# Loading token tile 1 of x from the ACT queue beside tile 0 on the SP queue

## The reference

```python
def rmsnorm(x, g):
    y = x * rsqrt(mean(x * x, -1) + EPS)
    return y * g

xn = rmsnorm(h, pool_norm[0])                # h is x, (256, 2048)
pooled = multiscale_pool(xn)                 # causal means over 2, 4, 8, 16 tokens, minus xn, per 512 columns
y = einsum('bsgc,gce->bsge', pooled, pool_w[0]) + pool_b[0]
h = h + y.reshape(B, S, D) * pool_scale[0]
h = h + swiglu(rmsnorm(h, ffn_norm[0]), w_gate[0], w_up[0], w_down[0])
```

## Time and profile before

| | |
|---|---|
| median of three runs | 1727.73 us (1726.87 to 1727.93) |
| the profiled execution, its own time | 1726.85 us |
| its span, first to last instruction | 1725.1 us |
| busy share of PE, DVE, ACT, POOL | 99%, 64%, 47%, 3% |
| DMA moved | 326.37 MB, mean 189 GB/s |

### The profile page before, as it was taken

How to read it: one execution, slowest core, us unless ns; L and a number is a source line. 1 busy time by engine, 2 the same in 40 slices (tenths; PEclk the granted TensorE clock), 3 DMA queues, 4 the chain that set the end, 5 groups by cost and what they waited for, 6 DMA issues and landing times. The chain is left out here.

```text
span 1725.1 us, 20840 instructions
## 1 busy us (share of the span) xinstructions
PE 1713.7 (99%) x7780; PEld 1413.2 (82%) x7780; DVE 1108.3 (64%) x1436; ACT 806.6 (47%) x1059; POOL 56.3 (3%) x65
## 2 busy tenths in 40 slices
PE   9999999999999999999999999999999999999998
PEld 8888888888888888888777788888888888888887
DVE  7666666666666646655676966666666666654554
ACT  6544444444444444446665554444444444443443
POOL 1100000000000000002010000000000000000000
PEclk9999999999999999999999999999999999999999
DMA  8555666555665565655444466666556555566562
GB/s 291 188 193 190 191 191 190 192 192 194 193 195 177 196 205 178 207 197 181 147 133 154 159 215 195 195 195 190 192 190 191 191 192 193 207 207 191 174 213 104
DMA packets 163162, 326.37 MB, mean 189 GB/s; under 512 B 5668, under 2 KB 5796, under 8 KB 162856
## 3 DMA queue, kind: packets, MB, share of 16 engines
q1 hardware_dynamic: 162960, 324.67, 57.4%
q10 hardware_dynamic: 152, 1.06, 0.2%
HBM read 323.61 MB, written 2.10 MB: 189 GB/s over the span
## 5 line engine op out<-in xcount | busy, mean ns | idle before, releaser
L656 DVE TENSOR_TENSOR w_lo<-raw,w_hi 128x1024 fp32r<-128x1024 f32 x584 | 702.3, 1207 | 529.2 <-ACT w_hi L349 525.5
L349 ACT ACTIVATE w_hi<-raw 128x1024 fp32r<-128x1024 f32 x584 | 605.3, 1038 | 788.3 <-PE acc L1064 784.1
L1062 PE MATMUL acc<-w_hi,xT_hi 128*128 128x512 f32 x1568 | 612.2, 390 | 0.0
L1064 PE MATMUL acc<-w_hi,xT_lo 128*128 128x512 f32 x1568 | 610.2, 389 | 0.0
L1063 PE MATMUL acc<-w_lo,xT_hi 128*128 128x512 f32 x1568 | 610.1, 389 | 0.0
L1062 PEld LDWEIGHTS acc<-w_hi,xT_hi 128*128 128x128 f32 x1568 | 294.4, 188 | 61.5
L1064 PEld LDWEIGHTS acc<-w_hi,xT_lo 128*128 128x128 f32 x1568 | 294.3, 188 | 61.3
L1063 PEld LDWEIGHTS acc<-w_lo,xT_hi 128*128 128x128 f32 x1568 | 294.4, 188 | 60.3
L1062 PE MATMUL acc<-w_hi,hT_hi 128*128 128x512 f32 x858 | 335.1, 391 | 1.2 <-DVE w_lo L656 1.1
L1064 PE MATMUL acc<-w_hi,hT_lo 128*128 128x512 f32 x858 | 333.9, 389 | 0.0
L1063 PE MATMUL acc<-w_lo,hT_hi 128*128 128x512 f32 x858 | 333.9, 389 | 0.0
(11 more groups left out here) (120 smaller groups left out, 441.1 us busy)
## 6 DMA issues: line engine op xcount, KB each, us to landing
raw<-w_gate_in SPq DMA_DIRECT2D x88, 1024.0 KB, 5.2
raw<-w_up_in SPq DMA_DIRECT2D x88, 1024.0 KB, 5.2
raw<-w_down_in SPq DMA_DIRECT2D x64, 1024.0 KB, 5.0
raw<-w_down_in SPq DMA_DIRECT2D x32, 768.0 KB, 4.3
raw<-w_q_in SPq DMA_DIRECT2D x16, 1024.0 KB, 5.1
raw<-w_o_in SPq DMA_DIRECT2D x16, 1024.0 KB, 5.1
raw<-w_kv_in SPq DMA_DIRECT2D x4, 1024.0 KB, 5.2
raw<-pool_w_in SPq DMA_DIRECT2D x3, 1024.0 KB, 13.2
```

The source lines that it names most:

```text
L349: nc.scalar.activation(w_hi[:, i % RING, 0:tiles * C], slot, ACT.Copy).then_inc(hi_ready, 1)
L656: nc.vector.tensor_tensor(w_lo[:, i % RING, 0:tiles * C], slot, w_hi[:, i % RING, 0:tiles * C].bitcast(F32), ALU.subtract).then_inc(unit_r ...
L1062: nc.tensor.matmul(dst, at_hi[:, k, tok], w_hi[:, w, cols], start=first and kk == 0, stop=False)
L1064: last = nc.tensor.matmul(dst, at_lo[:, k, tok], w_hi[:, w, cols], start=False, stop=end)
```

## The change

The SP queue keeps tile 0 of x, the first band and everything behind them. Tile 1's two pieces are issued by the ACT queue, ahead of the bias rows `vecs`. Semaphores, sizes and destinations stay as they are, and no waits are added or taken away.

```diff
         @block.sync
         def _(sp):
-            for t in range(T):
-                for half in range(2):
-                    cols = slice(half * D // 2, (half + 1) * D // 2)
-                    sp.dma_start(h[:, t, cols], x_v[:, t, cols]).then_inc(x_in[2 * t + half], 16)
-                if t == 0:
-                    sp.dma_start(band[:, 0:1, :], bands[:, 0:1, :]).then_inc(band0_in, 16)
+            for half in range(2):
+                cols = slice(half * D // 2, (half + 1) * D // 2)
+                sp.dma_start(h[:, 0, cols], x_v[:, 0, cols]).then_inc(x_in[half], 16)
+            sp.dma_start(band[:, 0:1, :], bands[:, 0:1, :]).then_inc(band0_in, 16)
             sp.dma_start(gains[:, :, :], gain_cols).then_inc(gains_in, 16)
...
+            for half in range(2):
+                cols = slice(half * D // 2, (half + 1) * D // 2)
+                nc.scalar.dma_start(h[:, 1, cols], x_v[:, 1, cols]).then_inc(x_in[2 + half], 16)
             nc.scalar.dma_start(vecs[:, :], pool_rows).then_inc(bias_in, 16)
 
             ac.wait_ge(consts_ready, 1)
```

## The result

The changed kernel took 1732.09 us (median of 10 runs, 1731.13 to 1732.64) against 1727.3 us before (10 runs, 1726.29 to 1727.93). The ratio is 1.0029, with a 95% interval of 1.0021 to 1.0037: 4.8 us slower. The profiled execution took 1731.47 us with a span of 1729.7, 4.6 us longer than the span before.

A forecast was written before the change was run, and what follows sets the result against it. TensorE, busy 1713.7 of 1725.1 us, was taken as the bound. First pool job 3.17 us late, less a 0.41 us gap, gave +2.8; the low clock's +2.0 made +4.8, so 1732.5 us, range 1729.7 to 1734.6.

The forecast's parts named there:

- SP's and ACT's issues at no cost: Kernel head: SP loses two issues, ACT gains two, 0.91 us per pair; both fall into slack and cost nothing.
- The bias lands at 9.0: ACT queue: the 8 KB bias load waits behind 1 MB of x and lands at 9.0, bounds 8.3 to 9.6.
- ScalarE's chain: Head: both tiles' squares follow the bias wait; vec_r 9.05, tile 0's root 11.89, first mix 12.85 instead of 8.65.
- The idle 1.0 us at 12.44 is absorbed and the 0.41 us gap closes: TensorE: the 1.03 us wait for later bands vanishes, as does a later 0.41 us gap, leaving +2.8 us.
- The clock: TensorE, idle 4 us before the first mix, drops to 1.2 GHz, slowing the mixes: +2.0 us, bounds 0 and 4.9.
- First pool job at 20.5: Sign in the timeline: the first pool job starts at 20.5 instead of 15.34, everything behind moved by one constant.
- how the queues share: Loading x: order of arrival puts tile 0 in by about 7.4, turns by packet near 8.8; both give +4.8 us.
- the bias load is not held up: Rival, ACT queue: the bias slips past or lands by 5; 0 to +0.7 us, about 1728; chance 0.11 including swallowed delay.
- faster: Rival, head: early bias and earlier bands win at most TensorE's 1.03 us of idleness, 1726.8 us; chance 0.03.
- swallowed by the pool stage: Rival: the DMA-bound pool stage, where ScalarE waits 3.5 us for weights, hides the delay: 0; chance 0.11 including early bias.
- the clock stayed: Rival: TensorE's clock stays at full through its idle time, so only +2.8 us, 1730.5; chance 0.13.
- stayed low for longer: Rival: TensorE's clock stays low longer or falls again during the slow mixes, up to +7.7 us, 1735.4; chance 0.08.

The follow-up runs named there:

- all on SP: Kernel before, x in its old order on the SP queue, bias load moved behind x on that queue: 1730.17 us, ratio 1.0016.
- bias step later: Changed kernel, loads unchanged, with the rounding of the bias rows and their rest moved behind tile 0's root and band: 1730.4 us, ratio 1.002.
- half on ACT: Changed kernel with only tile 1's second piece ahead of the bias load on the ACT queue, its first piece on SP: 1726.54 us, ratio 1.0001.

## Why the prediction was right

Its total, +4.8 us and 1732.5, met the measured +4.8 and 1732.09; on the scale of the profiled execution it had 1731.7 against 1731.47. By its steps:

- **SP's and ACT's issues at no cost:** right; in the new timeline nothing waits for a step that they moved, except through the order of the loads below.
- **The bias lands at 9.0:** it was 9.95, above the upper bound of 9.6. I had reckoned that x would come in no later than before; it took until about 10.4, with 0.99 MB moved from 3 to 7 us where one queue had moved 1.42. And the bias did not wait for all that was ahead of it in its queue: it was in use about 0.4 us before tile 1's last piece landed, and about 0.6 us before the last of x (issued at 2.7, 6.9 us to landing) in the kernel with the bias behind x on SP.
- **ScalarE's chain:** the order was as worked out, both tiles' squares after the bias. The steps were tighter than the spacings taken from the earlier trace rows: from vec_r to the first mix 3.46 us instead of 3.80. With the late landing the mix started at 13.41, not 12.85.
- **The idle 1.0 us at 12.44 is absorbed and the 0.41 us gap closes:** right. 1.11 us were given back there and 0.66 further on, where the gap was 0.41.
- **The clock:** fell as forecast after 4.5 us without work, for 3.4 us, at a price of 1.60 us where I took 2.0. The kernel with more warm-ups, 1.7 us shorter in its span, confirms this for the profiled execution. But that one is of the lower group. Six of the ten executions had a mean clock of 0.997, and the median is one of them; between the medians of the two kernels the clock's part is 2.4. The 2.0 lies between the two by luck.
- **First pool job at 20.5:** it was 20.59. Against the 20.51 of the sum, vec_r was +0.90 (9.95, not 9.05), the spacings to the first mix -0.34, the clock -0.40 and the tile 1 part -0.08. They nearly cancel, and that is luck.
- **The range:** the delay without the clock for the early bound, 2.8 - 0.7 = 2.1, gives 1729.8, where the text has 1729.7. Its upper end, 1734.6, follows from no sum in the text.

What was wrong is the step on how the queues share, and with it the rival "the bias load is not held up". I held tile 0 to be in by 7.4 or 8.8 and the bias to be later than either. In the changed kernel tile 0's second piece lands at about 10.2, beside the bias at 9.95. Either one alone would hold up the squares, and either one costs a good part of the loss: the bias alone +3.6 (all on SP), tile 0 alone +2.0 (bias first on SP) or +3.85 (bias rounded later, with the low clock in its profile). Much of the difference between these three is the clock. In the executions at 0.999 they cost +2.2, +1.9 and, in a single execution, +1.9; both together, in the changed kernel with more warm-ups, +3.15. So had the bias come early in the changed kernel, tile 0 alone would still have delayed the first mix by 3.49 of the 4.76 us (12.14 in the kernel with the bias step later, against 8.65). The prediction put all of it down to the bias. The +0.7 of that rival is too small for these two and too large for the kernel with the bias first on ACT. The Trainium skill, "DMA: Bandwidth & Descriptors", section "Queues, rings and completion order", has the engines take turns between queues a packet at a time; the even shares from 3 to 7 us agree with it., where one queue had the engines alone, stay unexplained; how they come about was not tried. The same page's "Issuing engines are not separate DMA queues" agrees too: tile 1's last piece was in at 9.73 with two queues and 9.54 with one.

The rivals "faster" and "swallowed by the pool stage" did not occur, and the clock stayed in none of the ten executions, by their means of 0.998 and 0.997. It may well have stayed low for longer, as another rival had it, in the six at 0.997, which cost 1.1 us more and not the 2.9 of that rival (+7.7 against +4.8); ScalarE's wait for pool weights vanished from the profile without saving TensorE anything.

## What to carry to other kernels

A second queue gave no bandwidth here, it changed the order: what was first in line shared the engines with what was second, and in the changed kernel both landed a little after the second used to (10.2 and 10.4 against 9.5). Before a load is put ahead of another in a queue, look for the small one behind it whose wait stands first in an engine's program. And when a delay leaves TensorE idle for some microseconds, add the pace of what follows, but only as far as no slack stands behind it.

## What I had not expected of the hardware

- Half a microsecond of head start goes with 3 us of landing. With the SP queue's x ahead of the ACT queue's by one issue, tile 0 was in at 7.24; with both at the same moment at 10.18 (the kernel with the bias step later, where ScalarE waited for it); with the ACT queue ahead at 9.96. The loads and their sizes are the same, but the bias load stands at another place in each, and each figure is from one profiled execution.
- A small load can be in before the large one ahead of it in its queue: the 8 KB of bias rows by about 0.4 us.
- The clock fell in one profiled execution about 1.1 us after the end of a pause of 2.25 us between matmuls (half on ACT) and held in another through one of 2.81 us (bias first, SP queue).
- Twenty warm-up products fewer cost the kernel before nothing, though its first mix took 1.94 us instead of 1.04.
